# Grouping the down product's steps between the transposes, and marking the next item's slots earlier, in a top-4-of-32 expert layer

## The reference

```python
logits = xf @ w_router + b_router
top_v, top_e = lax.top_k(logits, 4)            # 32 experts, 4 for each token
gates = jax.nn.softmax(top_v, axis=-1)
...                                            # tokens gathered by expert
gu = xb @ w_gu[e] + b_gu[e]                    # 1024 -> 2048
gate, up = gu[:, :1024], gu[:, 1024:]
gate = jnp.minimum(gate, 7.0)
up = jnp.clip(up, -7.0, 7.0)
h = (up + 1.0) * gate * jax.nn.sigmoid(1.702 * gate)
y = (h @ w_down[e] + b_down[e]) * gate_of_token
...                                            # added up by token
```

## Time and profile before

| | |
|---|---|
| median of 3 runs | 2765.6 us (2764.28 to 2765.81) |
| the profiled execution | 2765.81 us, its span 2764.0 us |
| PE busy | 2536.2 us, 92% |
| DVE busy | 1955.2 us, 71% |
| ACT busy | 1292.8 us, 47% |
| HBM | 182 GB/s over the span |

### The profile page before, as it was taken

How to read it: one execution, slowest core, us unless ns; L and a number is a source line. 1 busy time by engine, 2 the same in 40 slices (tenths; PEclk the granted TensorE clock), 3 DMA queues, 4 the chain that set the end, 5 groups by cost and what they waited for, 6 DMA issues and landing times.

```text
span 2764.0 us, 37900 instructions
## 1 busy us (share of the span) xinstructions
PE 2536.2 (92%) x11204; PEld 1809.1 (65%) x11205; DVE 1955.2 (71%) x3019; ACT 1292.8 (47%) x1840; POOL 355.2 (13%) x233
## 2 busy tenths in 40 slices
PE   7999986688989679999999999999999999999991
PEld 3544456356645357777777777777777777777770
DVE  0498978799723555666895769776877959657596
ACT  0331113333311134455774657564757747546473
POOL 0003711100020011010110211110201102001012
PEclk9999999679999679999999999999999999999995
DMA  4100020000020446567796869776877968757583
GB/s 152 61 4 31 0 107 1 1 1 1 3 82 1 175 165 190 183 211 245 275 361 197 279 207 350 279 257 204 309 244 276 361 199 310 243 178 280 191 310 143
DMA packets 81645, 488.49 MB, mean 177 GB/s; under 512 B 13683, under 2 KB 14963, under 8 KB 30454
## 3 DMA queue, kind: packets, MB, share of 16 engines
q1 hardware_dynamic: 66512, 449.67, 44.5%
q0 software_dynamic: 13104, 34.11, 5.7%
q10 hardware_dynamic: 1974, 4.02, 0.5%
HBM read 465.42 MB, written 36.70 MB: 182 GB/s over the span
## 4 chain that ended last, share of the span: by engine, by line
PE 66%; DVE 20%; issue 8%; DVEq 2%; DMA 2%; ACT 1%; POOLq 0%; POOL 0%; ACTq 0%; SPq 0%
PE ps L769 12%; PE ps L771 12%; PE ps L770 12%; DVE wlo L1471 10%; PE ps L519 7%; PE ps L530 5%; PE ps L694 4%; PE ps L790 3%; DVE score L1176 2%; PE ps L657 2%; PE ps L676 2%; DVE top L1175 2%; DVEq L369 2%; PE ps L800 1%; PE ps L548 1%
## 5 line engine op out<-in xcount | busy, mean ns | idle before, releaser
L1471 DVE TENSOR_TENSOR wlo<-raw,whi 128x1024 fp32r<-128x1024 f32 x776 | 932.7, 1221 | 273.9 <-ACT whi L1032 254.3
L1032 ACT ACTIVATE whi<-raw 128x1024 fp32r<-128x1024 f32 x776 | 817.8, 1060 | 440.8 <-PE ps L771 407.6
L769 PE MATMUL ps<-whi,xhi 128*128 128x512 f32 x1440 | 583.0, 405 | 0.0
L770 PE MATMUL ps<-wlo,xhi 128*128 128x512 f32 x1440 | 564.4, 392 | 0.0
L771 PE MATMUL ps<-whi,xlo 128*128 128x512 f32 x1440 | 562.0, 390 | 0.0
L769 PEld LDWEIGHTS ps<-whi,xhi 128*128 128x128 f32 x1440 | 270.7, 188 | 93.7 <-issue 41.0
L771 PEld LDWEIGHTS ps<-whi,xlo 128*128 128x128 f32 x1440 | 271.0, 188 | 59.1
L770 PEld LDWEIGHTS ps<-wlo,xhi 128*128 128x128 f32 x1440 | 271.2, 188 | 50.3
L769 PE MATMUL ps<-whi,hhi 128*128 128x512 f32 x720 | 298.9, 415 | 0.0
L1639 POOL DMA_INDIRECT acc<-ysb,idx_cur x45 | 130.9, 2909 | 1236.6 <-ACT ysb L1080 1232.6
L771 PE MATMUL ps<-whi,hlo 128*128 128x512 f32 x720 | 282.9, 393 | 0.0
(11 more groups left out here) (286 smaller groups left out, 2724.7 us busy)
## 6 DMA issues: line engine op xcount, KB each, us to landing
raw<-in_w_gu SPq DMA_DIRECT2D x260, 1024.0 KB, 6.7
raw<-in_w_dn SPq DMA_DIRECT2D x128, 1024.0 KB, 6.7
xT<-in_xT SPq DMA_DIRECT2D x2, 2048.0 KB, 15.9
raw<-in_w_out SPq DMA_DIRECT2D x2, 2048.0 KB, 9.7
h1all<-in_x SPq DMA_DIRECT2D x4, 1024.0 KB, 7.9
hext<-h1all SPq DMA_DIRECT2D x8, 512.0 KB, 12.0
acc<-accst SPq DMA_DIRECT2D x8, 512.0 KB, 2.6
fin<-acc SPq DMA_DIRECT2D x2, 2048.0 KB, 13.5
```

The costliest lines, as they stand in the source:

```text
L769: pe.matmul(bank_ap, hi, whi[:, slot, col, :], start=start, stop=False)
L770: pe.matmul(bank_ap, hi, wlo[:, slot, col, :], start=False, stop=False)
L1032: act.activation(whi[:, j % 2, 2 * g:2 * g + 2, :], raw[:, (j + 2) % 3, 2 * g:2 * g + 2, :], ACT.Copy)\
L1471: dve.tensor_tensor(wlo[:, j % 2, s, :], raw[:, (j + 2) % 3, s, :], whi[:, j % 2, s, :].bitcast(f32), ALU.subtract).then_inc(lo_done, 1)
```

## The change

On PE the eight steps of the down product are grouped anew. Before, one step stood between any two transposes from h3 on, and two behind x3. Now two steps stand behind h3 and two behind x0, one behind x1, one behind x2, and none behind x3. ACT and DVE take pieces and transposes in the matching order. On DVE `mark_slots` moves from the end of the item to the place behind `turned_lo` of h3.

```diff
--- before.py
+++ after.py
@@ -844,17 +844,17 @@
                 down(range(0, 2), i, n1, blocks)
                 turn_h(3, i, n1, blocks)
                 pe.wait_ge(tr_free[1], fill_of(i, "h", 1))
-                down(range(2, 3), i, n1, blocks)
+                down(range(2, 4), i, n1, blocks)
 
                 pe.wait_ge(tokens_in, i + 2)
                 turn(xg, (1, 0), 0, fill_of(i, "x", 0))
-                down(range(3, 4), i, n1, blocks)
+                down(range(4, 6), i, n1, blocks)
                 turn(xg, (1, 0), 1, fill_of(i, "x", 1))
-                down(range(4, 5), i, n1, blocks)
+                pe.wait_ge(tr_free[1], fill_of(i, "h", 3))
+                down(range(6, 7), i, n1, blocks)
                 turn(xg, (1, 0), 2, fill_of(i, "x", 2))
-                down(range(5, 6), i, n1, blocks)
+                down(range(7, 8), i, n1, blocks)
                 turn(xg, (1, 0), 3, fill_of(i, "x", 3))
-                down(range(6, 8), i, n1, blocks)
 
 
             find_slots(0, 1)
@@ -1062,15 +1062,14 @@
                 take_hi(6, (0, 1), i)
                 biases(ex)
                 turned_hi(hhi, 3, fill_of(i, "h", 3), len(blocks))
-                take_hi(6, (2,), i)
+                take_hi(6, (2, 3), i)
                 turned_hi(xhi, 0, fill_of(i, "x", 0))
-                take_hi(6, (3,), i)
+                take_hi(7, (0, 1), i)
                 turned_hi(xhi, 1, fill_of(i, "x", 1))
-                take_hi(7, (0,), i)
+                take_hi(7, (2,), i)
                 turned_hi(xhi, 2, fill_of(i, "x", 2))
-                take_hi(7, (1,), i)
+                take_hi(7, (3,), i)
                 turned_hi(xhi, 3, fill_of(i, "x", 3))
-                take_hi(7, (2, 3), i)
                 act.wait_ge(gate_cp, i + 1)
                 act.wait_ge(sum_kept, i + 1)
                 for b in blocks:
@@ -1507,16 +1506,15 @@
                         turned_lo(hhi, hlo, j - 1, fill_of(i, "h", j - 1, 0), len(blocks))
                 take_lo(6, (0, 1), i)
                 turned_lo(hhi, hlo, 3, fill_of(i, "h", 3, 0), len(blocks))
-                take_lo(6, (2,), i)
+                mark_slots(ex, i + 2, i + 3)
+                take_lo(6, (2, 3), i)
                 turned_lo(xhi, xlo, 0, fill_of(i, "x", 0, 0))
-                take_lo(6, (3,), i)
+                take_lo(7, (0, 1), i)
                 turned_lo(xhi, xlo, 1, fill_of(i, "x", 1, 0))
-                take_lo(7, (0,), i)
+                take_lo(7, (2,), i)
                 turned_lo(xhi, xlo, 2, fill_of(i, "x", 2, 0))
-                take_lo(7, (1,), i)
+                take_lo(7, (3,), i)
                 turned_lo(xhi, xlo, 3, fill_of(i, "x", 3, 0))
-                take_lo(7, (2, 3), i)
-                mark_slots(ex, i + 2, i + 3)
 
             starts(dve, gu_read)
             starts(dve, hb_done)
```

## The result

| | before | changed |
|---|---|---|
| median | 2764.9 us (2761.88 to 2765.81, 4 runs) | 2847.9 us (2845.75 to 2849.08, 4 runs) |
| profiled execution, span | 2765.81, 2764.0 us | 2841.84, 2840.0 us |
| ratio of the changed kernel to the one before | | 1.0299 [1.0286, 1.0311] |
| single item at full clock | 39.1 to 39.3 us | 41.6 to 41.9 us |
| double item at full clock | 73.8 us | 73.8 us |

The account below looks back on a forecast made before the run. PE bounds double items; a loop through DVE, PE and ACT sets single ones at 39.1 us. 2765.8 + 49 (boundaries 47.7, first passage 1) + 27 (clock) = 2842, given as 2840, range 2800 to 2859.

Parts of the forecast that it names:

- x1 no longer waits for h3: On PE in single items, x1 moves behind two steps, so its wait for h3's low half, 7.8 us over 19, disappears.
- The slots make x1's low half late, to S + 39.05: On DVE in single items, moved slots put x1's low half out 39.05 us after the item's start S; bound S + 40.3.
- PE waits 1.2 us ahead of x3: In single items PE reaches x3 at S + 37.8 and waits 1.2 us for x1's low half.
- PE's sequencer is held at x3: 2.7 us of loop code start only at S + 39.1, so the next bias product starts at S + 41.85; 47.7 us in all.
- The rival by which the code is hidden: PE's sequencer passes a waiting transpose, single items take 39.6 us, the kernel 2773; chance 0.12.
- Double items stay at 73.8: In double items DVE has room and the loop code is covered with 1 us to spare, so 73.8 us is unchanged.
- The clock falls at nearly all 18 boundaries, 27 us: Behind single items idle PE drops to half clock for 3.4 us, 1.5 us each, 27 us in all.
- The first boundary, 1 us: At the first passage of the loop, where PE already stood idle, 1 us is added once.
- the upper bound: For the falls of PE's clock behind single items, at most 18 by 1.7 us, 31 us.

Follow-up runs that it names:

- slots_alone: The kernel before with only `mark_slots` moved behind h3's low half on DVE, steps of the down product as before; 2796.2 us, ratio 1.0117.
- step7_behind_x3: The changed kernel with the last step of the down product behind x3 again; 2830.7 us, ratio 1.0244 to the kernel before.
- regroup_relv_early: The kernel before with the changed order of steps, slots last, and the subtraction for relv one piece earlier on DVE; 2780.9 us, ratio 1.0053.
- filler_behind_x3: The changed kernel with 16 extra unused products behind x3 on PE in single items; 2816.6 us, ratio 1.0196 to the kernel before.
- regroup_alone: The changed kernel with the slots put back at the end of DVE's item, steps still regrouped; 2794.3 us, ratio 1.0114 to the kernel before.
- relv_early: The kernel before with the subtraction for relv one piece earlier on DVE, ahead of piece (7,3), slots still last; 2741.4 us, ratio 0.9913.

## Why the prediction was right, point by point

- **x1 no longer waits for h3.** Right: the 7.8 us are gone. They were worth nothing by themselves, since another wait took their place.
- **The slots make x1's low half late, to S + 39.05.** Right to 0.1 us: 39.10 to 39.13 in items whose clock did not fall. What carried the number is that DVE is full from ACT's piece (5,2) on (busy for 14.33 of 14.40 us, 1361.9 to 1376.3, in an undisturbed item), and `slots_alone` shows the same chain by x0's half (40.2 us forecast and measured).
- **PE waits 1.2 us ahead of x3.** Right in the sum only: x0's half is late too, so PE waits some 0.4 us ahead of x2 and 0.8 ahead of x3. The working had no wait ahead of x2.
- **PE's sequencer is held at x3, and 2.4 to 2.7 us of code follow uncovered.** Right, and shown from five sides: line 864 within 0.1 us of the low half in every single item of the changed kernel, the undisturbed item of `step7_behind_x3`, the extra read that costs time in one kernel and none in the other's single items, `slots_alone` with its late half but two steps behind x3, and `regroup_relv_early` with an early half and none behind it. The rival by which the code is hidden fell: its 39.6 us were not seen with the changed kernel. It followed the rule of the Trainium skill (Advanced Engine Details and Errata, Sequencer Loop) that engine instructions are queued and wait there; for PE this case's sequencer rows say otherwise.
- **Double items stay at 73.8.** Right, at full clock. The cover was thinner than worked out: line 864 came 0.6 us behind the low half and not with it, and line 799 ended 0.6 to 0.9 us ahead of the item's end, where 1 us was forecast.
- **The clock falls at nearly all 18 boundaries, 27 us.** Right in kind: 16 of 18 boundaries behind single items in the profiled run. The term was too small, since seven of the 17 low stretches lasted 6.8 us and not 3.4. The profiled execution has some 31 us of it, the upper bound; the medians with `filler_behind_x3` give 34 to 36.
- **The first boundary, 1 us.** Small: items 0 and 1 took 2.5 us more, part of it a fall of the clock.

The sum was 2842 and the profiled execution 2841.84. That it came so close is luck: the loop grew by 80 us where 76 were forecast, and 4.1 us less outside it made up for that. In the loop the estimate is some 46 us for the 18 boundaries at full clock (forecast 47.7), 2.5 at the first boundary (1) and 31 for the clock (27). The other executions are at 2846 to 2849.

Several expectations of the experiments were off in size. For `regroup_alone` I took DVE's start in the item from the steady state of another kernel. For the two parts apart I gave too little to the clock. And an extra read of the table costs 0.45 us, where I had taken 0.73 from the distance of the two reads in the sequencer's rows. From line 864 to the end of line 799 the code grew by 0.5 to 0.6 us, and x1's low half came up to 0.1 us earlier in that kernel; why the read is shorter than 0.73 stays open.

## What to carry to other kernels

In a loop like this one, the last instruction ahead of the branch should be one that waits for nothing, with as much queued work behind the last wait as the sequencer needs for the loop's head; here 2.4 to 2.7 us on PE, and on DVE 3.8 from the start of the slots to the next piece. A wait there costs its own length plus what is left uncovered of that code, and the profile shows the code only as idle time put down to "issue". And before an operation is moved on an engine, see not its share over the span but whether it has any idle time in the stretch it moves into: DVE at 71% was full there, while the place it left was hidden under the sequencer's code.

## What the runs showed of the hardware that I had not expected

Extra work made a kernel faster: 16 short products in each of 19 items, 304 in all, took 31 us off, since some 2 us of idle PE behind 0.44 us of transposes and another 0.8 us of waiting had let the clock fall. A single wait of 2.0 us in otherwise dense products did it too, in 14 of 19 items of `slots_alone`, while the 1.7 us at the first boundary of the kernel before did not the earlier trace rows, and 2.3 us at the same place in `relv_early` did. And cutting one wait of DVE's sequencer on its own engine, for a result of 0.23 us of work, gave up to 0.9% of the whole kernel, 18 us of it in the loop.
